# Moving the first and last weight splits, the angles' range steps and the gating products of a convolution layer

## The reference, cut to what matters

```python
def hyena_filter_freq(L, w1, b1, w2, b2, w3, freq, decay):
    ...
    hid = jnp.sin(fr * (z @ w1.astype(f32) + b1.astype(f32)))
    hid = jnp.sin(fr * (hid @ w2.astype(f32) + b2.astype(f32)))
    h = (hid @ w3.astype(f32)).reshape(L, 2, HY_WIDTH)
    h = h * jnp.exp(-t[:, :, None] * jnp.abs(decay.astype(f32))[None])
    h_pos, h_neg = h[:, 0], h[1:, 1]
    norm = jnp.sqrt(jnp.sum(h_pos * h_pos, axis=0) + jnp.sum(h_neg * h_neg, axis=0))
    ...

def hyena(u, conv_w, conv_b, bias, filt):
    L = u.shape[1]
    x0, x1, v = jnp.split(short_conv(u, conv_w, conv_b), 3, axis=-1)
    z = v * x1
    hf = hyena_filter_freq(L, *filt)
    zf = jnp.fft.rfft(z.astype(jnp.float32), n=2 * L, axis=1)
    y = jnp.fft.irfft(zf * hf[None], n=2 * L, axis=1)[:, :L].astype(z.dtype)
    return x0 * (y + z * bias)
```

## Time and profile before

| | |
|---|---|
| median of 3 runs | 2417.89 us |
| the profiled execution | 2426.14 us |
| its span | 2424.2 us |
| TensorE busy | 2386.3 us, 98% |
| VectorE busy | 1610.2 us, 66% |
| ScalarE busy | 1192.7 us, 49% |
| GpSimd busy | 331.6 us, 14% |
| chain that ended last | TensorE 82%, VectorE 11%, ScalarE 3% |
| mean granted TensorE clock | 0.994 |

### The profile page before, as it was taken

How to read it: one execution, slowest core, us unless ns; L and a number is a source line. 1 busy time by engine, 2 the same in 40 slices (tenths; PEclk the granted TensorE clock), 3 DMA queues, 4 the chain that set the end, 5 groups by cost and what they waited for, 6 DMA issues and landing times.

```text
span 2424.2 us, 40267 instructions
## 1 busy us (share of the span) xinstructions
PE 2386.3 (98%) x17001; PEld 2189.1 (90%) x17001; DVE 1610.2 (66%) x2428; ACT 1192.7 (49%) x1977; POOL 331.6 (14%) x362
## 2 busy tenths in 40 slices
PE   8999999999999999999999999999999999999998
PEld 7999889999999998999997758878889888889998
DVE  5676676887777677678866865765653655466753
ACT  5445665544444567655554642421333444455643
POOL 1311002232132100035330001000001000001000
PEclk9999999999999999999999989999999999999999
DMA  7768634676676783466763211345542433334552
GB/s 238 228 224 221 201 109 135 219 237 208 217 241 224 208 224 121 123 200 223 244 200 108 55 46 53 122 166 182 189 158 87 150 104 105 120 117 146 179 195 96
DMA packets 374113, 401.54 MB, mean 166 GB/s; under 512 B 44708, under 2 KB 346048, under 8 KB 373677
## 3 DMA queue, kind: packets, MB, share of 16 engines
q1 hardware_dynamic: 371160, 391.19, 51.3%
q10 hardware_dynamic: 2772, 7.78, 1.0%
HBM read 397.87 MB, written 4.22 MB: 166 GB/s over the span
## 4 chain that ended last, share of the span: by engine, by line
PE 82%; DVE 11%; ACT 3%; issue 1%; POOL 1%; SPq 1%; DMA 0%; DVEq 0%; ACTq 0%; POOLq 0%
PE bank L685 25%; PE bank L687 24%; PE bank L686 24%; DVE rounded L2479 4%; PE bank L693 3%; DVE plain L2454 2%; ACT rounded L1670 2%; PE bank L698 1%; PE bank L1109 1%; PE bank L1139 1%; DVE plain L2464 0%; DVE plain L2712 0%; DVE plain L2752 0%; PE bank L1310 0%; ACT plain L2073 0%
## 5 line engine op out<-in xcount | busy, mean ns | idle before, releaser
L685 PE MATMUL bank<-rounded 128*128 128x256 f32 (+2 forms) x3480 | 1079.5, 310 | 7.5 <-DVE rounded L2479 2.9
L686 PE MATMUL bank<-rounded 128*128 128x256 f32 (+2 forms) x3480 | 1065.3, 306 | 0.0
L687 PE MATMUL bank<-rounded 128*128 128x256 f32 (+2 forms) x3480 | 1065.2, 306 | 0.0
L2479 DVE TENSOR_TENSOR rounded<-plain,rounded 128x1024 fp32r<-128x1024 f32 (+1 forms) x630 | 737.0, 1217 | 409.1 <-ACT rounded L1670 408.9
L1670 ACT ACTIVATE rounded<-plain 128x1024 fp32r<-128x1024 f32 (+1 forms) x630 | 616.4, 1032 | 359.1 <-PE bank L687 267.7
L685 PEld LDWEIGHTS bank<-rounded 128*128 128x128 f32 x3480 | 665.3, 191 | 53.5 <-issue 9.6
L687 PEld LDWEIGHTS bank<-rounded 128*128 128x128 f32 x3480 | 665.4, 191 | 29.0
L686 PEld LDWEIGHTS bank<-rounded 128*128 128x128 f32 x3480 | 665.7, 191 | 28.0
L685 PE MATMUL bank<-rounded,rounded 128*128 128x256 f32 (+2 forms) x1472 | 449.0, 305 | 5.7 <-DVE rounded L2479 2.3
L687 PE MATMUL bank<-rounded,rounded 128*128 128x256 f32 (+2 forms) x1472 | 445.4, 303 | 0.0
L686 PE MATMUL bank<-rounded,rounded 128*128 128x256 f32 (+2 forms) x1472 | 445.4, 303 | 0.0
(11 more groups left out here) (313 smaller groups left out, 1861.1 us busy)
## 6 DMA issues: line engine op xcount, KB each, us to landing
plain<-in_mlp_w SPq DMA_DIRECT2D x64, 1024.0 KB, 5.3
plain<-in_ada_w SPq DMA_DIRECT2D x48, 1024.0 KB, 5.5
plain<-in_ffn_w_gate SPq DMA_DIRECT2D x44, 1024.0 KB, 5.7
plain<-in_ffn_w_up SPq DMA_DIRECT2D x44, 1024.0 KB, 5.5
plain<-in_ffn_w_down SPq DMA_DIRECT2D x32, 1024.0 KB, 5.6
plain<-in_w_in SPq DMA_DIRECT2D x32, 1024.0 KB, 5.4
plain<-in_od_w_in SPq DMA_DIRECT2D x32, 1024.0 KB, 5.4
plain<-in_ffn_w_down SPq DMA_DIRECT2D x16, 768.0 KB, 6.3
```

Of the source, the lines that this page charges most:

```text
L685: pe.matmul(dst, a[0], b[0], start=first and i == 0, stop=False)
L686: pe.matmul(dst, a[0], b[1], start=False, stop=False)
L687: ins = pe.matmul(dst, a[1], b[0], start=False, stop=last and i == n - 1)
L2479: dve.tensor_tensor(low, raw, top, SUB).then_inc(*done(("lo", m, half)))
```

## The change

Four things change, all in `even`. (1) The split of unit kv+3 (`hi` on ScalarE, `lo` on VectorE) stood before the first softmax and stands behind it. The last split in the rounds (the third unit behind the last convolution's, wo2) stood behind convolution 11; now `hi` stands behind the second row transposes' copies and `lo` behind the even and odd parts. (2) `size`, the absolute values of the decays, leaves the slot list and runs on ScalarE behind the transposed weights of round 11. (3) Of an angle, VectorE keeps the step that reads PSUM; the range steps run on GpSimd as nine instructions (a multiply and an add in place of each of the three joint ones), and the four gating products run there too, in the order 2, 3, angle 0, angle 1, 6, 7. (4) VectorE adds the four squared planes to one in two additions, TensorE's power takes 4 matmuls in place of 16, and stands within the second spectrum.

```diff
@@ -657,7 +657,7 @@
 WINDOW = [[0, None, 256, 128], [384, 256, 128, 0]]
 
 BESIDE = [("conv", 0)] + [slot for i in range(12) for slot in (
-    ("conv", i + 1) if i < 11 else None, {2: ("net", 0), 4: ("net", 1), 8: ("decays", 0), 10: ("size", 0)}.get(i))]
+    ("conv", i + 1) if i < 11 else None, {2: ("net", 0), 4: ("net", 1), 8: ("decays", 0)}.get(i))]
 def tensor_program(pe, L, M):
     at, new, done, here, U = M.marks.at, L.new, L.done, L.here, M.U
     hx, part = M.hx, M.part
@@ -1279,10 +1279,10 @@
         def power():
 
             b = bank(s, "rn")
-            for x in new(at(s, "hsq")):
+            for x in new(at(s, "hsum")):
                 pe.wait_ge(*x)
             for j in range(4):
-                ins = plain(b[:, j:j + 1], [(b_.Hh[:, a, j * 128:j * 128 + 128], M.ones[:, 0:1]) for a in range(4)])
+                ins = plain(b[:, j:j + 1], [(b_.Hh[:, 0, j * 128:j * 128 + 128], M.ones[:, 0:1])])
             ins.then_inc(*done((s, "rn")))
 
         def beside(n):
@@ -1345,6 +1345,8 @@
 
         def spectrum(q):
             for kc in range(2):
+                if q and kc:
+                    power()
                 for a, mat in enumerate((b_.cm, b_.sm)):
                     b = bank(s, "zf", q, kc, a)
                     for x in new(at(s, "zk", q, 0), at(s, "zk", q, 1)):
@@ -1393,7 +1395,6 @@
             for a in range(2):
                 response(kc, a)
         spectrum(1)
-        power()
         back(0)
         bs0 = [bank(s, "wo", j) for j in range(2)]
         for k in range(4, 8):
@@ -2121,7 +2122,6 @@
         for x in new(at(s, "vt")):
             act.wait_ge(*x)
         act.activation(a_.PT[0], M.bank(s, "vt")[:, :], ACT.Copy, scale=1.0).then_inc(*done((s, "vt", "s"), ("free", s, "vt")))
-        hi(U[s, "kv"] + 3)
 
         def convolve(n):
 
@@ -2133,7 +2133,7 @@
                 act.wait_ge(*x)
             act.activation(o, M.bank(s, "cv", n)[:, :], ACT.Identity, bias=col("hy_conv_b_2", c),
                            scale=col("conv_w", 12 + c)).then_inc(*done((s, "cu", n)))
-            if jj:
+            if jj and n < 11:
                 hi(U[s, "cv", part, blk] + 3)
 
         def hidden(n):
@@ -2184,8 +2184,6 @@
                 hidden(x)
             elif kind == "decays":
                 decays()
-            else:
-                size()
 
         def weights(x):
             kind = b_.jobs[x][0]
@@ -2194,6 +2192,7 @@
 
         n = len(b_.jobs)
         weights(0)
+        hi(U[s, "kv"] + 3)
         beside(0)
         for x in new(at(s, "v")):
             act.wait_ge(*x)
@@ -2203,6 +2202,7 @@
             if i + 1 < n:
                 weights(i + 1)
             else:
+                size()
                 for d in range(2):
                     decayed(0, d)
             if i and BESIDE[2 * i] is not None and BESIDE[2 * i][0] == "net":
@@ -2225,6 +2225,7 @@
         for d in range(2):
             decayed(1, d)
         byrows(1)
+        hi(U[s, "cv", 0, 1] + 3)
         spectrum(0)
         for x in new(at(s, "PN")):
             act.wait_ge(*x)
@@ -3082,7 +3083,6 @@
             lo(U[s, "q", jj] + 3)
         turned(3)
         turned(4)
-        lo(U[s, "kv"] + 3)
 
         def convolve(n):
             part, blk, jj = CONV[n]
@@ -3098,32 +3098,14 @@
                 dve.wait_ge(*x)
             dve.scalar_tensor_tensor(o2[:, :, 0:255], u2[:, :, 1:256], col("conv_w", 24 + c), o2[:, :, 0:255], MUL,
                                      ADD).then_inc(*done((s, "cvd", n), ("free", s, "cv", n)))
-            if part == 2:
-                for x in new(L.last()):
-                    dve.wait_ge(*x)
-                dve.tensor_tensor(b_.z[:, j, :], b_.z[:, j, :], b_.x1[:, jj, :], MUL).then_inc(*done((s, "cvo", 2, j), (s, "x1")))
 
         def hidden(n):
 
-            a, r_, bias = b_.hd[n][0:64, :], b_.zf[0:64, :], ("hy_b1_2", "hy_b2_2")[n]
+            a, bias = b_.hd[n][0:64, :], ("hy_b1_2", "hy_b2_2")[n]
             for x in new(at(s, "hy", n)):
                 dve.wait_ge(*x)
             dve.tensor_scalar(a, M.bank(s, "hy", n)[0:64, 0:256], col(bias)[0:64, :], col("hy_freq_2")[0:64, :], ADD,
-                              MUL).then_inc(*done(("free", s, "hy", n)))
-            for x in new(L.last()):
-                dve.wait_ge(*x)
-            dve.tensor_scalar(r_, a, float(1 / (2 * np.pi)), 12582912.0, MUL, ADD).then_inc(*done())
-            for x in new(L.last()):
-                dve.wait_ge(*x)
-            dve.tensor_scalar(r_, r_, 12582912.0, None, SUB).then_inc(*done())
-            c1, c2 = 6.28125, 0.0019350051879882812
-            for c in (c1, c2, float(2 * np.pi - c1 - c2)):
-                for x in new(L.last()):
-                    dve.wait_ge(*x)
-                dve.scalar_tensor_tensor(a, r_, -c, a, MUL, ADD).then_inc(*done())
-            for x in new(L.last()):
-                dve.wait_ge(*x)
-            dve.tensor_scalar(a, a, 3.1415925, -3.1415925, ALU.min, ALU.max).then_inc(*done((s, "ang", n)))
+                              MUL).then_inc(*done((s, "arg", n), ("free", s, "hy", n)))
 
         def taps(tile, d):
             for x in new(at(s, "tap", tile, d), at(s, "tw", tile, d)):
@@ -3233,6 +3215,7 @@
         n = len(b_.jobs)
         first(0)
         then(0)
+        lo(U[s, "kv"] + 3)
         beside(0)
         for i in range(n):
             if i + 1 < n:
@@ -3243,7 +3226,7 @@
                 byrows(0)
             if i:
                 beside(2 * i)
-                if CONV[i][2]:
+                if CONV[i][2] and i + 1 < n:
                     lo(U[(s, "cv", *CONV[i][0:2])] + 3)
             beside(2 * i + 1)
             kept(i)
@@ -3252,6 +3235,13 @@
             for d in range(2):
                 taps(tile, d)
             evenodd(tile)
+        lo(U[s, "cv", 0, 1] + 3)
+        for x in new(at(s, "hsq")):
+            dve.wait_ge(*x)
+        dve.tensor_tensor(b_.Hh[:, 0:2, :], b_.Hh[:, 0:2, :], b_.Hh[:, 2:4, :], ADD).then_inc(*done())
+        for x in new(L.last()):
+            dve.wait_ge(*x)
+        dve.tensor_tensor(b_.Hh[:, 0, :], b_.Hh[:, 0, :], b_.Hh[:, 1, :], ADD).then_inc(*done((s, "hsum")))
         for q in range(2):
             for kc in range(2):
                 filtered(q, kc)
@@ -3613,6 +3603,40 @@
         for c in range(1, 8, 2):
             rest(s, c, 0, c)
         here(s, "begun", "pool")
+
+        def gated(n):
+            blk, jj = CONV[n][1:]
+            j = 2 * blk + jj
+            for x in new(at(s, "cvd", n)):
+                pool.wait_ge(*x)
+            pool.tensor_tensor(b_.z[:, j, :], b_.z[:, j, :], b_.x1[:, jj, :], MUL).then_inc(*done((s, "cvo", 2, j)))
+
+        def angle(n):
+            a, r_, t_ = b_.hd[n][0:64, :], b_.zf[0:64, :], b_.hd[1 - n][0:64, :]
+            for x in new(at(s, "arg", n)):
+                pool.wait_ge(*x)
+            pool.tensor_scalar(r_, a, float(1 / (2 * np.pi)), 12582912.0, MUL, ADD).then_inc(*done())
+            for x in new(L.last()):
+                pool.wait_ge(*x)
+            pool.tensor_scalar(r_, r_, 12582912.0, None, SUB).then_inc(*done())
+            c1, c2 = 6.28125, 0.0019350051879882812
+            for c in (c1, c2, float(2 * np.pi - c1 - c2)):
+                for x in new(L.last()):
+                    pool.wait_ge(*x)
+                pool.tensor_scalar(t_, r_, -c, None, MUL).then_inc(*done())
+                for x in new(L.last()):
+                    pool.wait_ge(*x)
+                pool.tensor_tensor(a, a, t_, ADD).then_inc(*done())
+            for x in new(L.last()):
+                pool.wait_ge(*x)
+            pool.tensor_scalar(a, a, 3.1415925, -3.1415925, ALU.min, ALU.max).then_inc(*done((s, "ang", n)))
+
+        gated(2)
+        gated(3)
+        angle(0)
+        angle(1)
+        gated(6)
+        gated(7)
         for x in new(at(s, "attended", "pe"), at(s, "attended", "act"), at(s, "attended", "dve"), at(s, "turned", "pe")):
             pool.wait_ge(*x)
         for c in range(6):
```

## The result

| | before | the change |
|---|---|---|
| median | 2419.34 us (11 runs, 2416.68 to 2421.29) | 2424.53 us (11 runs, 2422.06 to 2425.06) |
| the profiled execution | 2426.14 us | 2424.68 us |
| ratio to before | | 1.0018, 95% interval 1.0010 to 1.0026 |

The change is slower by 0.18%, some 4 to 5 us, where 5 us of gain were forecast; the time lies just above the range. That it lies beside rival (1)'s 2423.8 is chance, since that rival wanted a chain of 12.6 us. Note the second row: in the two profiled executions the order is the other way round. The profile of before is 6.8 us above that kernel's median, the profile of the change is on its own.

The account below looks back on a forecast made before the run. TensorE, busy 98% of the span, was taken as the bound. Terms -1.4 + 6.6 + 1.5 - 2.1 - 2.6 - 10.2 + 1.7 + 1.2 = -5.3 us on the median 2417.9 gave 2412.6 us, range 2405 to 2424.

Parts of the forecast that it names:

- rival (1): Angles: one-input GpSimd steps cost more than a copy, chain 12.6 us, sum +5.9, 2423.8 us; chance 0.16.
- The head: First softmax: with the split behind it, TensorE's 1.1 and 0.3 us waits before the first transposes go; -1.4 us.
- the end of the attention: Before the last wait: copies and absolute decays move behind the transposed weights, removing TensorE's 2.1 us wait; -2.1 us.
- the norm: Filter's power sum: 4 matmuls in place of 16, 24 fewer records; -2.6 us at the full clock.
- A = 6 x 0.5 + 3 x 0.74 + 9 x 0.15 + 0.4 = 7.0 us: GpSimd's chain per angle: six one-input, three two-input steps, nine hand-overs, 0.4 us conflict with VectorE; ends 5.2 and 16.7.
- 2A - 7.4: Both angles: TensorE's added delay as a function of GpSimd's chain length A; +6.6 us for A of 7.0 us.
- the prediction's own sign of being wrong: Profile after: a GpSimd one-input duration over 0.9 us would prove the forecast wrong.
- rival (2): Angles: VectorE's differences and GpSimd hold each other, chain 9.0 us, sum -1.3, 2416.6 us; chance 0.12.
- "+1.5 us, an estimate": Behind both angles' waits of 3.9 and 4.6 us: each brings a lower-clock stretch in place of one of 3.4 us.
- "-6.8 - 3.4 = -10.2 us": Taps and norm: the second and third lower-clock stretches lose their causes and go; -10.2 us.
- "as I sum differences I put them on the median": Whole kernel: differences from the profiled execution (2426.1 us), 8.2 us above the median, applied to median 2417.9, giving 2412.6 us.
- The give-back of 1.7 us: Taps: one 3.4 us lower-clock stretch stays, since they use 64 of 128 rows; +1.7 us, ends 0 and 6.8.

Follow-up runs that it names:

- e4: The change with the two split differences beside each angle's first step moved behind that round's convolution sums; 2425.81 us in a single execution.
- e1: The kernel before, unedited, profiled a second time; 2418.82 us.
- e12: The kernel before, unedited, profiled a third time; 2417.98 us.
- e2: The change with the angles' range steps back on VectorE, all else as changed; 2409.85 us, ratio to before 0.9945.
- e5: The change with each sine one round later on ScalarE and the network's second layer one round later, range steps still on GpSimd; 2406.45 us, ratio to before 0.995.
- e7: The kernel before with only the last split and the absolute decays (size) moved; 2415.29 us, ratio to before 0.9979.
- e9: The change with the subtraction joined to each product in GpSimd's chain, 8 steps; 2423.77 us, ratio to before 1.0007.
- e10: e5 with the range steps on VectorE; 2410.21 us, ratio to before 0.9951.
- e11: e5 with the joined subtract-and-product steps of e9 on GpSimd; 2408.2 us, ratio to before 0.9944.

## Why the prediction was wrong

**What bounds the kernel, and the moves.** Right: TensorE waits only at the places of the earlier trace rows, and each of the other moves did to its wait what was said. The head is -1.8 us against -1.4, the end of the attention -2.2 against -2.1, the norm has 8 records of 0.9 us, and the new wait for the filter product is 1.24 us against 1.2.

**The angles**, "A = 6 x 0.5 + 3 x 0.74 + 9 x 0.15 + 0.4 = 7.0 us". The form 2A - 7.4 held, the term 0.4 us for conflict did not: the two differences of the split, which the change puts beside the first step, held GpSimd for 2.0 us (e4). A was 9.2, of the 2.2 us too much 1.6 from that term. The other 0.6 us are the single steps: 0.85 us for a subtraction or a product alone and 0.40 for the two-operation steps, a mean of 0.70 where 0.5 was taken, less a hand-over of 0.09 where 0.15 was. A one-input step of over 0.9 us was the prediction's own sign of being wrong. TensorE's waits behind the two sines were 4.6 and 5.8 us, where 3.9 and 4.6 were forecast. This was rival (2), with its 9.0 us; it had 0.12.

**"+1.5 us, an estimate"** for the lower clock behind the longer waits. Its length was mis-sized: 10.2 and 6.8 us, where one stretch of 3.4 had been before. Its cost was not, between these two profiles: 2A - 7.4 is 11.0 us for the measured A, and the stretch of the angles took 11.8 more, so some 0.8 us are left for the clock. Much of it lay in time in which TensorE waits for VectorE anyway. Beside e1 and e12, which had no lower clock at 1374 us, the same stretch is 13.4 us longer (85.7 for 72.3).

**"-6.8 - 3.4 = -10.2 us"** for the clock, and with it "as I sum differences I put them on the median". This is the larger of the two steps that failed. Against the profiled execution it was right: the last stretch gave -11.2 us against -9.9, the difference being mostly the 1.7 us of give-back. But that execution was 8.2 us above the median shown, which the prediction explained as "spread over the kernel". It was not spread: the lower clock over the taps was 13.6 us long in it and 3.4 us in e1 and e12, a difference of 5.1 us, and the 3.4 us at 1374 were missing in both, another 1.7. Those 6.8 us are as much as separates the profile of before (2426.14) from its median (2419.34). How much lower clock the median run has was not measured, but a gain that only removes what it has not got is no gain on the median.

In the prediction's terms, -5.3 us, +6.8 for that clock and +3.7 for the angles (11.8 for 8.1) make +5.2; neither error alone would have moved the time by more than 2 us from before (+1.5 and -1.6). The other three stretches of the stage came out 0.4, 0.1 and 1.3 us better than forecast, which leaves +3.4. The traces say +5.0 and +3.3 us for the stage, beside e1 and e12, and the medians +5.2 for the whole. Of the 11.9 us between 2412.6 and 2424.53 another 1.4 are the median of before, 2417.89 of 3 runs and 2419.34 of 11. So the sign and the size are accounted for to about 2 us; what is left lies ahead of scores 0 or in which executions had how much lower clock, and stays open.

**The give-back of 1.7 us** for 64-row taps at the full clock: nothing was given back. In the change, e2, e4, e5, e7, e9, e10 and e11, none of which has the 2.1 us wait, the clock did not fall over the taps.

## What to carry to other kernels

Before you price a clock stretch or a stall out of a profile, compare that execution's time with the median: if they differ, find the stretch that makes the difference and take it out of the account. An instruction that waits for a slow helper engine costs what is queued behind it, not its own length: here the same nine steps cost 14 us ahead of a copy that others needed, and nothing one round later. And put nothing that reads two SBUF operands on VectorE beside a short GpSimd step that others wait for.

The version to keep is e5: 2406.45 us, 0.5% under before and 0.7% under the change.

## What the runs showed of the hardware

- GpSimd on 64x256 float32 from SBUF: multiply and add with two constants 0.40 us, minimum and maximum 0.39, a subtraction alone 0.85, a product alone 0.84, subtraction and product joined 1.07, an addition of two tensors 0.73. More operations in one instruction did not mean more time: multiply and add took half of either a subtraction or a product alone, subtract and multiply more than either. On VectorE the multiply and add, the subtraction and the minimum and maximum took 0.28 us each.
- GpSimd's first step took 2.44 us beside two VectorE instructions with two SBUF inputs (2.35 us together), and 0.40 us without them (e4, and angle 1 of e5): it let both of them through.
- One program on one core, with the same waits, was at the lower clock for 13.7 us over the taps in some executions and for 3.4 us in others, a difference of 5 us in its time. The eight records of the taps took 3.70 us in e7 without the wait, 3.84 in e12 behind it, where the clock was up again 0.3 us into them, and 7.19 in the earlier trace rows, where it stayed down through them.
